# Writing out TensorE's loop over pairs of experts while the other engines keep theirs

## The chip, the cores and the metric

The kernel runs on one core of a Trainium2 chip. Five engines work side by side, each with its own list of instructions: TensorE (PE) multiplies, the vector engine (DVE), the scalar engine (ACT) and GpSimd (POOL) do elementwise work, and SyncE (SP) issues the DMA transfers. They wait for each other by semaphores. The metric is the device time of one execution in microseconds (us), as the median of several runs.

## The reference: what is computed

One inference step of a decoder with two layers, on 256 prompt tokens and 8 sample tokens (264 columns). Layer 0 is a state-space mixer and a dense SwiGLU; layer 1 is windowed attention and a mixture of experts. The change lies in the mixture alone, which takes most of the time:

```python
def moe_swiglu(h, w_router, w_gu, w_down):
    logits = jnp.einsum('btd,de->bte', h, w_router, preferred_element_type=jnp.float32)
    top_v, top_i = lax.top_k(logits, TOP_K)            # 2 of 8
    gates = jax.nn.softmax(top_v, axis=-1)
    comb = ...                                          # gates spread over the 8 experts
    for e in range(N_EXPERTS):
        out = out + comb[..., e:e + 1] * swiglu(h, w_gu[e], w_down[e])
```

The model width is 1024, an expert's hidden width 3584, everything is in 32-bit floats.

## The kernel before, in words

Each float of a weight is split into a high part (ACT's cast, line 662) and a low part (DVE's subtraction, line 1204), and TensorE makes three passes (lines 1715 to 1717) in place of one. Weights come in tiles of 128 x 2048 floats (1 MB): 51 for everything before the experts (the dense stage), then 42 for each of 8 experts, 28 for gate and up and 14 for down. SP loads a tile into one of six raw buffers once the tile six before it has been split (line 336, the function `load`). ACT casts it once TensorE has used the tile three before it (semaphore `used`), DVE subtracts after each half of the cast (`hi_made`), and TensorE multiplies after each half of the subtraction (`tiles_split`).

An expert works on at most 128 tokens. The tokens of two experts are gathered together (`gather`, line 1944, by matrices that DVE makes), which is why experts go in pairs. Then come seven blocks j of 4 tiles each for gate and up; after the second tile of block j TensorE transposes the activations of block j-1 (`turn`, line 1957). Then come 14 tiles of the down product. The result is added to the residual by `scatter` (line 1970), eight matmuls after the second and eight after the fourth tile of the next expert's block 0.

`expert_rest(r, half, more, next_pair)` is one expert from its block 1 on, and ends with block 0 of expert r+1 with the scatter of r in it. So the first block of expert 0 stands ahead of everything, and a pass of the pair loop begins at block 1 of an even expert. Its end, the border spoken of below, lies between the last scatter matmul of block 0 and the first product of block 1. The stage is three passes of that loop (experts 0 to 5), and the last pair written out after it. TensorE (line 2030), ACT (line 908) and DVE (line 1499) each have this loop for themselves; SP has one over single experts (line 349). The engines are tied by semaphores only, nothing makes them meet at a loop's end. A semaphore's target in the stage is worked out in a register from the expert's number r, by `snap`. If an expert has over 128 tokens, a further loop behind the stage takes the rest (line 2037); it is jumped over here.

In the dense stage TensorE has a smaller loop (line 1751), three passes of six tiles with 48 matmuls each.

Of the kernel before, what the change touches and what calls it, by code (L numbers as in the profile page):

```python
# [52 lines left out]
E, DFE = 8, 3584  # L53
# [26 lines left out]
def build(nc, xT, xu, gu, vecs, wd, we, wr, a_re, a_im, log_dt, bq, bx, cq, cx, h0q, h0x,  # L80
          kcT, vc, sinks, relb, onehot,
          yT, hp_out, hs_out, kp_out, vp_out, ks_out, vs_out):
    with ExitStack() as ctx:
# [7 lines left out]
        def sem(name):  # L91
            if name not in sems:
                sems[name] = ctx.enter_context(nc.semaphore(name))
            return sems[name]
# [176 lines left out]
        def expert_tile(r, m):  # L271
            return (r, NE, NDENSE + m)
# [1253 lines left out]
        def _(pe):  # L1526
# [293 lines left out]
            def turn(u):  # L1820
                pe.wait_ge(sem("p_ready"), u + 1)
                pe.wait_ge(sem("p2_ready"), heads_upto(u))
                if u >= 2:
                    pe.wait_ge(sem("pt_ready"), u - 1)
                for i in range(3 if UNITS[u] < NH else 1):
                    mm = t_.transpose(ps[:, 2 + u % 2, i * P:(i + 1) * P], SC[:, u % 3, i * P:(i + 1) * P], ident[:, :])
                mm.then_inc(sem("p_turned"), 1)
# [109 lines left out]
            def gather(r, i, experts):  # L1937

                if i == 0:
                    pe.wait_ge(sem("dispatched"), pe.snap(r * 3 + 3 * experts))  # L1940
                for c in range(2):
                    for t in range(3):
                        for part in (HTH, HTL):
                            mm = t_.matmul(ps[:, i, c * 2 * P:(c + 1) * 2 * P],  # L1944
                                           part[:, t, (2 * i + c) * P:(2 * i + c + 1) * P], DSP[:, t, :],
                                           start=(t == 0 and part is HTH), stop=(t == 2 and part is HTL))
                mm.then_inc(sem("gathered"), experts)
# [13 lines left out]
            def scatter(r, i):  # L1961

                if i == 0:
                    pe.wait_ge(sem("ye_split"), pe.snap(r + 1))
                    pe.wait_ge(sem("gs_made"), pe.snap(r + 1))
                else:
                    pe.wait_ge(sem("x_added"), pe.snap(r * 2 + 2))
                for c in range(4 * i, 4 * i + 4):
                    for y in (YEH, YEL):
                        mm = t_.matmul(ps[:, 4 + c % 4, 0:NT], y[:, c * P:(c + 1) * P], GSH[:, :],  # L1970
                                       start=(y is YEH), stop=(y is YEL))
                mm.then_inc(sem("scattered"), 1)

            def product(tile, stat, bank, first, last):

                w = WH[tile[2] % SPLIT], WL[tile[2] % SPLIT]
                for k in range(2):
                    pe.wait_ge(split, at(pe, tile, 1, 2) if k else half_of(pe, tile))
                    for i in range(2):
                        cols = slice((2 * k + i) * 512, (2 * k + i + 1) * 512)  # L1980
                        mm = passes(ps[:, bank + i, :], stat[k], [x[:, cols] for x in w],
                                    first and k == 0, last and k == 1)
                mm.then_inc(used, 1)

            def expert_gate_up(r, j, half, experts=0, prev=None):
                if j >= 2:
                    pe.wait_ge(sem("act_ready"), pe.snap(r * JE + (j - 1)))
                slots = slice(half * P, (half + 1) * P)
                for kq in range(4):
                    if experts and j == 0 and kq:  # L1990
                        pe.wait_ge(sem("xel_ready"), pe.snap(r * 4 + experts * (kq + 1)))
                    elif experts and j == 0:
                        pe.wait_ge(sem("xel_ready"), pe.snap(r * 4 + experts * 2))
                    product(expert_tile(r, 4 * j + kq), [[x[:, 2 * kq + k, slots] for x in (XEH, XEL)] for k in range(2)],
                            2 * (j % 2), kq == 0, kq == 3)
                    if kq == 1 and j:
                        turn(r, j - 1)
                    if prev is not None and kq % 2:
                        scatter(prev, kq // 2)

            def expert_rest(r, half, more, next_pair=False):
                for j in range(1, JE):
                    expert_gate_up(r, j, half)
                for d in range(NDE):
                    if d % 2 == 0:
                        pe.wait_ge(sem("af_split"), pe.snap(r * JE + (d // 2 + 1)))
                    product(expert_tile(r, NGU + d), [[x[:, 2 * d + k, :] for x in (AFH, AFL)] for k in range(2)],
                            4, d == 0, d == NDE - 1)
                    if d == 1:
                        turn(r, JE - 1)  # L2010
                    if d == 3:

                        pe.wait_ge(sem("af_split"), pe.snap(r * JE + (JE - 1)))
                        pe.wait_ge(sem("gate_spread"), pe.snap(r * 3 + 3))
                        for t in range(3):
                            mm = t_.transpose(ps[:, 7, t * P:(t + 1) * P], DG[:, t, :], ident[:, :])
                        mm.then_inc(sem("gate_turned"), 1)
                    if 5 <= d < 9 and next_pair:
                        gather(pe.snap(r + 1), d - 5, 2)
                if more:  # L2020
                    expert_gate_up(pe.snap(r + 1), 0, 1 - half, 2 if next_pair else 0, r)
                else:
                    scatter(r, 0)
                    scatter(r, 1)

            zero = pe.snap(0)
            for i in range(4):
                gather(zero, i, 2)
            expert_gate_up(zero, 0, 0, 2)
            with pe.Fori(0, E // 2 - 1) as p:  # L2030
                expert_rest(pe.snap(p * 2), 0, True)
                expert_rest(pe.snap(p * 2 + 1), 1, True, True)
            expert_rest(pe.snap(zero + (E - 2)), 0, True)
            expert_rest(pe.snap(zero + (E - 1)), 1, False)
            pe.wait_ge(sem("plan_ready"), 1)
# [90 lines left out]
```

## Time and profile before

| what | value |
|---|---|
| median of 3 runs | 1606.36 us (1605.78 to 1606.58) |
| profiled execution | 1608.89 us, span 1606.8 us |
| TensorE busy | 1506.1 us, 94% |
| TensorE weight loads busy | 1275.2 us, 79% |
| DVE busy | 1257.1 us, 78% |
| ACT busy | 999.1 us, 62% |
| data read from HBM | 415.31 MB, 263 GB/s over the span |
| mean granted TensorE clock | 0.969 |

A profile is one execution; its span runs from the first to the last instruction. PE are the matmuls and PEld the weight loads that overlap them; PEldq, DVEq and ACTq are what an engine's sequencer handles by itself, such as register operations and branches. Times in rows are us from the span's start unless marked ns. The duration of a matmul is longer than the distance to the next, since matmuls are pipelined; distances are read from starts. "[3.65 <-DVE WL L1204]" is the idle time of the engine ahead of an instruction, and what the profile takes for its end.

### The profile page before, as it was taken

How to read it: one execution, taken by the hardware profiler on the slowest of the kernel's cores; microseconds unless marked ns; L12 is line 12 of the kernel's file. 1: busy time of each engine (PE TensorE's matmuls, PEld its weight loads, DVE VectorE, ACT ScalarE, POOL GpSimd, SP SyncE). 2: the span in 40 equal slices, each digit the busy share in tenths (PEclk: the TensorE clock that was granted, in tenths of full speed). 3: DMA queues.
4: the chain of work that ended last, by engine and by line, in shares of the span. 5: the costliest groups of instructions: out<-in, count | busy, mean ns of one | idle time of the engine just before them, and what ended most of it. 6: DMA issues, size and time to landing. Idle time of an engine off the chain costs nothing.

```text
span 1606.8 us, 23615 instructions
## 1 busy us (share of the span) xinstructions
PE 1506.1 (94%) x8293; PEld 1275.2 (79%) x8294; DVE 1257.1 (78%) x1532; ACT 999.1 (62%) x1315; POOL 121.1 (8%) x143
## 2 busy tenths in 40 slices
PE   2799989999898899999999999999999999999995
PEld 1788989999777688888878888887888888888884
DVE  7964565554566489899979989988989989999983
ACT  4444444433456467777757777776777777777772
POOL 3982003000100000000000000000000000000000
PEclk9798999999899999999999999999999999999997
DMA  2005588445413259999988999988999988999980
GB/s 103 27 1 200 204 131 309 177 171 183 152 58 139 79 227 362 368 354 364 348 308 324 360 366 351 360 312 311 361 370 346 363 328 336 361 367 356 364 320 28
DMA packets 61948, 423.68 MB, mean 264 GB/s; under 512 B 8302, under 2 KB 8454, under 8 KB 11665
## 3 DMA queue, kind: packets, MB, share of 16 engines
q1 hardware_dynamic: 58784, 412.37, 67.7%
q0 software_dynamic: 3056, 9.85, 3.0%
q8 instruction: 69, 1.13, 0.3%
q14 instruction: 39, 0.32, 0.1%
HBM read 415.31 MB, written 6.88 MB: 263 GB/s over the span
## 4 chain that ended last, share of the span: by engine, by line
PE 89%; DVE 7%; ACT 2%; issue 1%; DMA 0%; SPq 0%; DVEq 0%; ACTq 0%
PE ps L1715 26%; PE ps L1717 26%; PE ps L1716 26%; PE ps L1944 2%; PE ps L1957 2%; PE ps L1532 1%; PE ps L1596 1%; PE ps L1970 1%; PE ps L1627 1%; PE ps L1628 1%; PE ps L1568 1%; DVE XN L978 0%; ACT TM L625 0%; PE ps L1576 0%; DVE AM L1081 0%
## 5 line engine op out<-in xcount | busy, mean ns | idle before, releaser
L1204 DVE TENSOR_TENSOR WL<-raw,WH 128x1024 fp32r<-128x1024 f32 x774 | 908.0, 1222 | 120.7 <-ACT WH L662 120.0
L662 ACT CAST WH<-raw 128x1024 fp32r<-128x1024 f32 x774 | 772.3, 1047 | 176.4 <-PE ps L1717 176.3
L1715 PE MATMUL ps<-WH,XEH 128*128 128x512 f32 x896 | 361.1, 403 | 7.3 <-DVE WL L1204 7.3
L1717 PE MATMUL ps<-WH,XEL 128*128 128x512 f32 x896 | 353.3, 394 | 0.0
L1716 PE MATMUL ps<-WL,XEH 128*128 128x512 f32 x896 | 352.8, 394 | 0.0
L1715 PEld LDWEIGHTS ps<-WH,XEH 128*128 128x128 f32 x896 | 168.7, 188 | 44.1 <-DVE WL L1204 7.8
L1717 PEld LDWEIGHTS ps<-WH,XEL 128*128 128x128 f32 x896 | 169.1, 189 | 42.9
L1716 PEld LDWEIGHTS ps<-WL,XEH 128*128 128x128 f32 x896 | 169.0, 189 | 36.7
L1715 PE MATMUL ps<-WH,AFH 128*128 128x512 f32 x448 | 178.8, 399 | 0.0
L1717 PE MATMUL ps<-WH,AFL 128*128 128x512 f32 x448 | 176.7, 394 | 0.0
L1716 PE MATMUL ps<-WL,AFH 128*128 128x512 f32 x448 | 176.6, 394 | 0.0
L1715 PE MATMUL ps<-XNH,WH 128*128 128x264 f32 x496 | 145.7, 294 | 9.7 <-DVE XNL L973 9.7
L1716 PE MATMUL ps<-XNL,WH 128*128 128x264 f32 x496 | 143.6, 290 | 0.0
L1717 PE MATMUL ps<-XNH,WL 128*128 128x264 f32 x496 | 143.5, 289 | 0.0
L1715 PEld LDWEIGHTS ps<-XNH,WH 128*128 128x128 f32 x496 | 96.6, 195 | 10.8 <-issue 10.5
L1717 PEld LDWEIGHTS ps<-WH,AFL 128*128 128x128 f32 x448 | 84.1, 188 | 20.8
L1716 PEld LDWEIGHTS ps<-WL,AFH 128*128 128x128 f32 x448 | 84.2, 188 | 18.9
L1715 PEld LDWEIGHTS ps<-WH,AFH 128*128 128x128 f32 x448 | 84.2, 188 | 18.9
L1716 PEld LDWEIGHTS ps<-XNL,WH 128*128 128x128 f32 x496 | 96.8, 195 | 0.2
L1717 PEld LDWEIGHTS ps<-XNH,WL 128*128 128x128 f32 x496 | 96.2, 194 | 0.0
L871 ACT CAST AFH<-ps 128x512 fp32r<-128x512 f32 x56 | 32.9, 587 | 67.7 <-PE ps L1957 67.7
L723 ACT ACTIVATE SG<-ps 128x264 f32<-128x264 f32 x30 | 11.7, 390 | 91.7 <-PE ps L1717 91.6
(368 smaller groups left out, 1772.2 us busy)
## 6 DMA issues: line engine op xcount, KB each, us to landing
raw<-in_we SPq DMA_DIRECT2D x336, 1024.0 KB, 5.3
raw<-in_wd SPq DMA_DIRECT2D x51, 1024.0 KB, 4.8
bias_rows<-SC POOLq DMA_DIRECT2D x1, 3072.0 KB, 35.7
BIAS<-bias_rows POOLq DMA_DIRECT2D x16, 128.0 KB, 9.7
U<-in_xu SPq DMA_DIRECT2D x1, 1280.0 KB, 7.8
X<-in_xT SPq DMA_DIRECT2D x1, 1056.0 KB, 10.7
out_yT<-XN SPq DMA_DIRECT2D x2, 528.0 KB, 2.7
out_ks<-KCT POOLq DMA_DIRECT2D x1, 1024.0 KB, 9.3
```

The lines of the kernel that those rows point to most:

```text
L662: a.copy(WH[tile[2] % SPLIT][:, cols], raw[slot_][:, cols]).then_inc(sem("hi_made"), 1)
L871: a.copy(AFH[:, 4 * j:4 * j + 4, :], ps[:, 6 + j % 2, :].rearrange("p (c n) -> p c n", c=4))\
L1204: v.tensor_tensor(WL[tile[2] % SPLIT][:, cols], raw[tile[2] % RING][:, cols], WH[tile[2] % SPLIT][:, cols].bitcast(F32), ALU.subtract).the ...
L1532: t_.matmul(ps[:, NORM_BANK[i], 0:NT], ones[:, :], SQ[:, c % 2, :], start=(c == 0), stop=(c == KC - 1))\
L1568: mm = t_.matmul(ps[:, 6 + b % 2, g * UC:(g + 1) * UC], AT[:, 4 * (b % 2) + g, :], U[:, hf * GH + 4 * b + g, :], start=True, stop=True)
L1596: mm = t_.matmul(ps[:, 2 + b % 2, g * P:(g + 1) * P], AM[:, hf * GH + 4 * b + g, :], CM[hf][:, 4 * b + g, :], start=True, stop=True)
L1627: t_.matmul(out, U[:, 4 * u + g, :], TM[hf][:, k, :], start=True, stop=False)
L1715: t_.matmul(out, sh, mh, start=first, stop=False)
L1716: t_.matmul(out, sh, ml, start=False, stop=False)
L1717: return t_.matmul(out, sl, mh, start=False, stop=last)
L1944: mm = t_.matmul(ps[:, i, c * 2 * P:(c + 1) * 2 * P], part[:, t, (2 * i + c) * P:(2 * i + c + 1) * P], DSP[:, t, :], start=(t == 0 and par ...
L1957: mm = t_.transpose(ps[:, 6 + j % 2, i * P:(i + 1) * P], AC[:, j % 2, i * P:(i + 1) * P], ident[:, :])
```

## The change: the loop is written out on TensorE

```diff
@@ -2027,9 +2027,9 @@
             for i in range(4):
                 gather(zero, i, 2)
             expert_gate_up(zero, 0, 0, 2)
-            with pe.Fori(0, E // 2 - 1) as p:
-                expert_rest(pe.snap(p * 2), 0, True)
-                expert_rest(pe.snap(p * 2 + 1), 1, True, True)
+            for p in range(E // 2 - 1):
+                expert_rest(pe.snap(zero + 2 * p), 0, True)
+                expert_rest(pe.snap(zero + (2 * p + 1)), 1, True, True)
             expert_rest(pe.snap(zero + (E - 2)), 0, True)
             expert_rest(pe.snap(zero + (E - 1)), 1, False)
             pe.wait_ge(sem("plan_ready"), 1)
```

`pe.Fori` is a loop that runs on the engine's sequencer, with a counter in a register and a jump back at its end. The Python loop writes its body three times into TensorE's list. `zero` is a register that holds 0. TensorE executes the same matmuls and waits in the same order; ACT, DVE and SP are as they were.

## Rows read from the trace of the kernel before

**Rows 1.** The page, part 4: the chain that ended last, by engine.

```profile
PE 89%; DVE 7%; ACT 2%; issue 1%; DMA 0%; SPq 0%; DVEq 0%; ACTq 0%
```

**Rows 2.** Waits of PE, 572 to 1590 us: total us, times, longest.

```profile
PE ps L1715 <- DVE WL L1204: 7.3, 2, 3.7
PE ps L1970 <- DVE YEL L1465: 2.5, 1, 2.5
PE ps L1970 <- DVE X L1445: 1.4, 1, 1.4
```

**Rows 3.** Timeline of PE, first pass's end: start, us, instruction, idle before.

```profile
833.98 0.28 PE L1970 MATMUL ps<-GSH,YEL 128*128 128x264 f32 x1
837.91 0.49 PE L1715 MATMUL ps<-WH,XEH 128*128 128x512 f32 x1 [3.65 <-DVE WL L1204]
...
845.14 0.60 PE L1957 MATMUL ps<-ident,AC 128*128 128x128 f32 x4
```

**Rows 4.** The same at the second pass's end.

```profile
1090.37 0.28 PE L1970 MATMUL ps<-GSH,YEL 128*128 128x264 f32 x1
1094.34 0.62 PE L1715 MATMUL ps<-WH,XEH 128*128 128x512 f32 x1 [3.69 <-DVE WL L1204]
...
1101.57 0.60 PE L1957 MATMUL ps<-ident,AC 128*128 128x128 f32 x4
```

**Rows 5.** The same at the third pass's end, and two later tiles' first matmuls.

```profile
1346.84 0.28 PE L1970 MATMUL ps<-GSH,YEL 128*128 128x264 f32 x1
1346.95 0.39 PE L1715 MATMUL ps<-WH,XEH 128*128 128x512 f32 x1
...
1352.53 0.60 PE L1957 MATMUL ps<-ident,AC 128*128 128x128 f32 x4
...
1355.76 0.39 PE L1715 MATMUL ps<-WH,XEH 128*128 128x512 f32 x1
...
1358.54 0.39 PE L1715 MATMUL ps<-WH,XEH 128*128 128x512 f32 x1
```

**Rows 6.** Line 2030, TensorE's pair loop: ns min/median/max, first and last start.

```profile
L2030 PEldq COMPARE_BRANCH  x3: 83/5919/5973, 831.8 to 1344.7; - x3
```

**Rows 7.** Busy time by stretch: us, PE, PEld, DVE, ACT, POOL, PEclk, DMA share, GB/s.

```profile
838.50:841.90 3.40, 3.40 (x10) 2.65 (x9) 0.00 (x0) 0.00 (x0) 0.00 (x0) 0.51 0.80 304
1352.50:1580.00 227.50, 226.79 (x1015) 183.42 (x1013) 202.86 (x188) 167.34 (x185) 0.00 (x0) 1.00 0.86 332
846.00:1090.00 244.00, 244.00 (x1117) 198.94 (x1117) 222.01 (x218) 182.53 (x206) 0.00 (x0) 1.00 0.92 350
```

**Rows 8.** Timeline of PE, the first pass's first transposes.

```profile
588.73 0.60 PE L1957 MATMUL ps<-ident,AC 128*128 128x128 f32 x4
```

**Rows 9.** DMA queues, 834 to 1090, then 1346 to 1580: transfers, MB, share.

```profile
q8 instruction: 12, 0.20, 0.3%
...
q8 instruction: 8, 0.13, 0.2%
```

**Rows 10.** Line 1751, TensorE's loop in the dense stage, as in rows 6.

```profile
L1751 PEldq COMPARE_BRANCH  x3: 83/220/247, 248.0 to 317.6; - x3
```

**Rows 11.** Timeline of ACT, first cast behind the first and third border.

```profile
842.55 2.00 ACT L662 CAST WH<-raw 128x1024 fp32r<-128x1024 f32 x2 [6.74 <-PE ps L1717]
...
1349.99 2.00 ACT L662 CAST WH<-raw 128x1024 fp32r<-128x1024 f32 x2 [1.32 <-PE ps L1717]
```

**Rows 12.** Line 1499, DVE's pair loop, in 836:842 and in 1092:1098.

```profile
L1499 DVEq COMPARE_BRANCH  x1: 63/63/63, 836.0 to 836.0; - x1
L1499 DVEq FUSED_REGOPS  x1: 80/80/80, 840.3 to 840.3; - x1
...
L1499 DVEq FUSED_REGOPS  x1: 74/74/74, 1096.6 to 1096.6; - x1
```

**Rows 13.** Timeline of DVE behind the third border, next three tiles (two halves each).

```profile
1351.20 2.35 DVE L1204 TENSOR_TENSOR WL<-raw,WH 128x1024 fp32r<-128x1024 f32 x2
...
1354.73 4.73 DVE L1204 TENSOR_TENSOR WL<-raw,WH 128x1024 fp32r<-128x1024 f32 x4 [0.25 <-ACT WH L662]
```

## The prediction

> **What bounds the kernel now.** I read the page's chain of waits first: 89% of the span is TensorE, 7% DVE [rows 1], so only what shortens TensorE's own line of matmuls can shorten the kernel. Then the list of waits, cut to the expert stage and to TensorE, for what interrupts that line: three entries, 11.2 us in all, of some 1,000 us [rows 2]. Two of the interruptions, 7.3 us together, stand before line 1715, at the first matmul of a tile; the other two (2.5 and 1.4 us) are the exposed last scatter of the last expert, which the change does not touch.
>
> The timeline shows where the two are. The last scatter matmul of the first pass starts at 833.98 and the next matmul at 837.91, 3.93 us later; in the second pass it is 1090.37 and 1094.34, 3.97 us [rows 3, 4]. The same place at the end of the third pass, where the loop is left by falling through, has 1346.84 and 1346.95: 0.11 us [rows 5]. The same instructions, the same queues; the loop's jump back is what two of the three have. The rows of line 2030, the loop itself, say it directly: three branches on TensorE's sequencer, of 83, 5919 and 5973 ns (minimum, median, maximum) [rows 6]. The sequencer reaches the branch ahead of the array (at 831.8 by that view), so some 2 us of the 5.9 pass under matmuls already queued and the rest is the gap. The profile's releaser, DVE's WL, is only the last semaphore that this tile waited for, given long before: in the third pass the same wait costs nothing.
>
> There is a second price. [...] So I measure an edge not by its gap but from the last scatter matmul to the first group of transposes (line 1957), two tiles later, when the clock is back: 845.14 - 833.98 = 11.16 us, 1101.57 - 1090.37 = 11.20 us, and without a jump 1352.53 - 1346.84 = 5.69 us [rows 3 to 5]. An edge costs 5.47 and 5.51 us, 10.98 us together, of which 3.82 and 3.86 are the gap and 1.65 each the slow clock.
>
> Is any of it made good later, so that it would not be a gain? From the transposes to the next pass's last scatter the kernel takes 833.98 - 588.73 = 245.25 us in the first pass (no jump ahead of it), 1090.37 - 845.14 = 245.23 in the second and 1346.84 - 1101.57 = 245.27 in the third [rows 3 to 5, 8]. Nothing is made good: the stall comes off whole.
>
> **The change, part by part.** Removed: TensorE's two taken jumps. By the above 10.98 us, all on the path. The third branch (83 ns, not taken) and the loop's counter go too; the sequencer runs ahead there (the gap is 0.11 us), so nothing.
>
> Added: the expert number as `zero + 2p` instead of `2p`. It stays a register, and every wait goes on being computed from it; the last pair has this form already and runs at TensorE's pace: its stretch from 1352.5 to 1580 has 226.79 us of 227.50 busy at clock 1.00 [rows 7]. Nothing, with no visible end on either side but the 0.7 us of that row for a whole pair.
>
> Moved: the instructions come from new code instead of from the same code again. Both are fetched anyway. The second pass of the loop has 12 transfers of the instruction queue q8, the straight last pair 8 in a stretch a little shorter (1346 to 1580 against 834 to 1090) [rows 9]. TensorE runs 288 matmuls in a pass of the dense loop (line 1751), about 1,150 in a pass of this one; only this one pays at its edge, while that loop's branches take 83 to 247 ns [rows 10]. The large loop is read anew in each pass, so writing it out adds no transfers worth a term, and straight code crosses from one transfer to the next without a gap in [rows 7]. Bounds: nothing, or for some 20 transfers in two passes up to the 0.7 us of the last pair each time, 1.4 us. I take nothing, since the passes of 245.2 us contain such transfers and agree to 0.04 us.
>
> What is late next. ACT and DVE keep their loops, and TensorE's pause covered their jumps. ACT: its first cast behind the first border starts at 842.55 after 6.74 us of idle time, put down to TensorE, which frees the buffer; in the third pass the same cast waits 1.32 us for the same [rows 11]. Hence ACT's jump costs between 0 and 6.7 us, and up to 1.3 us of it are hidden in any case; I take it as hidden, since TensorE explains the idle time by itself. DVE is the tighter one. Its branch is at 836.0 and its loop's next instruction, the counter's, at 840.3; in the second pass the counter is at 1096.6, 6.2 us behind the last scatter as against 6.3 us [rows 12, 3, 4]. So its jump costs 4.2 us, and it can start the next WL at some 840.3 + 0.1 - 833.98 = 6.4 us behind the last scatter, where in the third pass it starts at 1351.20 - 1346.84 = 4.36 us [rows 13, 5]: 2.1 us later. Its slack in the third pass: that WL's first half is there at 1351.20 + 1.2 = 1352.4 and TensorE wants it at 1355.76 (the tile's first matmul), 3.3 us; the next tile's at 1354.73 + 1.2 = 1355.9 against 1358.54, 2.6 us [rows 5, 13]. With 2.1 us gone 1.2 and 0.5 us remain, and TensorE doesn't wait. If the whole slack were gone, each us more of DVE's jump would be a us of TensorE; from below the cost is nothing. I take 0.1 us for each edge, for a fetch a little slower when TensorE's loads run on beside it.
>
> SP: with no pause its loads follow without one. A stretch of 244 us between two borders runs at a DMA share of 0.92, the last pair at 0.86 [rows 7], and TensorE, which would be the last to feel a late load, waits for nothing in them [rows 2]. Nothing; if loads did fall behind in a longer run, it would be a loss of the same kind as DVE's, below.
>
> At the end the branch of line 2037 and the final norm stand as before, behind all this.
>
> Sum against the profiled execution (1608.89 us): 10.98 - 0.2 = 10.8 us less, 1598.1 us. The median shown, 1606.36, is 2.53 us below the profiled one; on it the forecast is 1595.6 us.
>
> **The rivals.**
> DVE's loop edge takes over in part. For: DVE is busy 202.86 us of 227.5 [rows 7] and can't catch up fast; its slack is 0.5 us by my count. Against: the half us is there. Price: were its jump as long as TensorE's 5.97 us instead of 4.2, the 1.75 us more would exceed the 0.5 by 1.2 us, at two edges 2.5 us. Time 1606.36 - 10.98 + 2.5 = 1597.9 us; with TensorE's clock falling again after such a wait (1.65 each) 1601.2.
>
> The change doesn't remove what costs: the gap is the wait for WL, as the profile's releaser says, and the jump is cheap, as at the dense loop's edge (0.25 us at most [rows 10]). Then two jumps save at most 0.5 us: 1605.9 us. For it speak the releaser and those branches. Against it: the third pass, and branches of 5.9 us in [rows 6]. [...]
>
> Slower: TensorE's unbroken run grows from some 480 us (1101.6 to the end, at clock 1.00 [rows 7]) to some 1,000 us. If the granted clock fell to half somewhere in it, each us there would cost half a us; it decides from 28 us at half clock on (10.98 + 3.2, doubled). At 40 us: 1606.36 - 10.98 + 20 = 1615.4 us. Nothing in the trace hints at it: the only falls in this stage follow a standstill.
>
> **How the numbers follow.** About 0.2%, 3.2 us, is what a measurement of this kernel can tell from no change. The forecast 0.86; DVE's edge in part 0.07; the jump not the cause 0.04; slower by the clock 0.02; a mixture that loses over half the gain 0.01. The first two, and half of the last, are faster by over 0.2%: 0.94; within 0.2%: 0.04; slower: 0.02. Range: down to 1593.6 (the gain whole, and 1.8 us for another run's level; the three runs of before span 0.8 us), up to 1599.6 (beyond DVE's case, 1597.9). The other signs hold too little chance to widen it.
>
> **What the changed kernel's profile would show.** At the pair borders, near 834, 1085 and 1336 us, the next matmul 0.1 us behind the last scatter and the transposes at 5.7 us, with no clock below 1.00 there: the term of 10.98. TensorE's waits in the stage down to the two of the last expert, 3.9 us. No branch rows on its sequencer at the loop. DVE still with its jump of 4.2 us, its next WL at about 6.4 us, and TensorE's tile at 8.9 us without a wait: the term of 0.1. I am wrong if gaps of us stay at those borders (the cause was the data), if TensorE waits two or three tiles behind them (DVE's edge), if gaps appear every 20 us within a pair (fetching), or if the clock falls in mid-run.

## The result, and the profile after

The changed kernel takes 1594.35 us in the median (1593.03 to 1595.24, four runs) against 1606.47 us, 12.1 us less: a ratio of 0.9921, 95% interval 0.9908 to 0.9934, which is 10.6 to 14.8 us. (The ratio, here and below, is an estimate of its own; that of the two medians would be 0.9925.) The forecast was 1595.6 us. The profiled execution took 1593.03 us with a span of 1590.9, against 1608.89 and 1606.8 before.

The chain of waits of the page is as before. TensorE's waits between 572 and 1580 us, the columns as in [rows 2], no longer hold an entry for line 1715; the two of the last expert's scatter are left (the first line is the final norm, behind the stage).

```profile
PE ps L1532 <- ACT SQ L534: 4.6, 1, 4.6
PE ps L1970 <- DVE YEL L1465: 2.5, 1, 2.5
PE ps L1970 <- DVE X L1445: 1.3, 1, 1.3
```

TensorE's timeline at the first border answers to [rows 3], and below it the one stretch of busy time (columns as in [rows 7]) that spans the whole stage.

```profile
828.96 0.28 PE L1970 MATMUL ps<-GSH,YEL 128*128 128x264 f32 x1
829.08 0.39 PE L1715 MATMUL ps<-WH,XEH 128*128 128x512 f32 x1
...
834.65 0.60 PE L1957 MATMUL ps<-ident,AC 128*128 128x128 f32 x4
```

```profile
567.00:1563.00 996.00, 996.00 (x4538) 810.99 (x4536) 904.36 (x884) 740.18 (x828) 0.00 (x0) 1.00 0.92 346
```

The border takes 5.69 us where [rows 3] have 11.16; at the second it is 1085.57 - 1079.87 = 5.70 us. TensorE is busy for 996 of 996 us at a granted clock of 1.00. The loop's rows of line 2030 are gone with the loop, and q8, the queue of the instructions, moves 63 transfers in the whole kernel in place of 69.

DVE's side of the first border, its timeline and the rows of its loop, answers to [rows 12, 13]:

```profile
832.16 1.25 DVE L1445 TENSOR_TENSOR X<-ps,X 128x1056 f32<-128x1056 f32 x1
835.27 2.36 DVE L1204 TENSOR_TENSOR WL<-raw,WH 128x1024 fp32r<-128x1024 f32 x2 [1.85 <-issue]
```

```profile
L1499 DVEq COMPARE_BRANCH  x1: 62/62/62, 831.0 to 831.0; - x1
L1499 DVEq FUSED_REGOPS  x1: 80/80/80, 835.1 to 835.1; - x1
```

Its next WL starts 835.27 - 828.96 = 6.31 us behind the last scatter, now with its own jump ("issue") named for the idle time and no longer ACT, and TensorE does not wait for it.

A measure without the scatter of whole runs. The profiles' spans differ by 15.9 us, more than the medians. The difference lies in two parts: ahead of the expert stage, where no instruction was changed, and in it. The first and last start of TensorE's gather (line 1944) and scatter (line 1970), in ns min/median/max and us, for the kernel before and then for the changed one:

```profile
L1944 PE MATMUL ps<-DSP,HTH x96: 276/283/582, 564.0 to 1319.7; 128*128 128x256 f32 x96
L1970 PE MATMUL ps<-GSH,YEL x64: 278/284/425, 698.4 to 1586.3; 128*128 128x264 f32 x64
```

```profile
L1944 PE MATMUL ps<-DSP,HTH x96: 276/283/582, 559.1 to 1303.6; 128*128 128x256 f32 x96
L1970 PE MATMUL ps<-GSH,YEL x64: 278/283/422, 693.4 to 1570.1; 128*128 128x264 f32 x64
```

From the first gather to the last scatter, "the stage" from here on, the kernel before takes 1586.3 - 564.0 = 1022.3 us and the changed one 1570.1 - 559.1 = 1011.0: 11.3 us. Another 564.0 - 559.1 = 4.9 us stand ahead of it, where the mean granted clock of the first 558 us is 0.94 before and 0.96 after; behind the last scatter the changed kernel takes 0.3 us more.

### The profile page after: what moved, and what is told of

Same layout as the page of the kernel before. It is cut to its first block, busy times and chain, and to the rows that moved or that the text cites. A ratio compares the mean times of both kernels' runs of the same rounds, so it can differ in the third digit from the quotient of the medians.

```text
span 1590.9 us, 23128 instructions
## 1 busy us (share of the span) xinstructions
PE 1496.5 (94%) x8293; PEld 1267.1 (80%) x8294; DVE 1256.6 (79%) x1532; ACT 999.5 (63%) x1315; POOL 121.5 (8%) x143
## 4 chain that ended last, share of the span: by engine, by line
PE 89%; DVE 7%; ACT 3%; issue 1%; DMA 0%; SPq 0%; DVEq 0%; ACTq 0%
PE ps L1715 26%; PE ps L1717 26%; PE ps L1716 26%; PE ps L1944 2%; PE ps L1957 2%; PE ps L1532 1%; PE ps L1970 1%; PE ps L1596 1%; PE ps L1627 1%; PE ps L1628 1%; PE ps L1568 1%; DVE XN L978 0%; ACT TM L625 0%; DVE SV L1113 0%; PE ps L1576 0%
## 5 line engine op out<-in xcount | busy, mean ns | idle before, releaser
L662 ACT CAST WH<-raw 128x1024 fp32r<-128x1024 f32 x774 | 772.3, 1047 | 165.2 <-PE ps L1717 165.1
L1715 PEld LDWEIGHTS ps<-XNH,WH 128*128 128x128 f32 x496 | 95.6, 193 | 11.3 <-issue 10.5
```

Of the source, the lines that this page charges most:

```text
L662: a.copy(WH[tile[2] % SPLIT][:, cols], raw[slot_][:, cols]).then_inc(sem("hi_made"), 1)
L1715: t_.matmul(out, sh, mh, start=first, stop=False)
```

## The experiments

The stage's length is given for each from the same two rows of its own profile, beside the timed median. All ratios are to the kernel before, timed anew beside each group of experiments: 1606.81 us for the first four, 1607.07 us for the four with a hint, with far jumps or with a placed head, 1606.41 us for the other four.

**The changed kernel once more.** No edit.

> The changed kernel once more, beside the others on the same chip. The forecast was 10.8 us less than before, the first measurement 12.1 us (ratio 0.9908 to 0.9934, 10.6 to 14.8 us). Theory A (the two jumps of TensorE cost 5.5 us each and nothing else changed; the rest of the first profile's 15.9 us is scatter of the granted clock ahead of the expert stage): 1595.5 us, a saving of 10.5 to 12 us, and a profile whose time between the first gather and the last scatter is 11 us shorter than before's, wherever the stage starts. Rival B (something ahead of the expert stage got faster too, through the new layout of TensorE's code): a saving of 13 us or more, and the stage starting at 567 us again in the profile, not at 572.

Measured: 1595.42 us (1592.16 to 1595.54), ratio 0.9922, interval 0.9910 to 0.9935: a saving of 11.4 us between the medians, 12.5 us by the ratio. The stage takes 1569.4 - 558.5 = 1010.9 us. It starts at 558.5 here, and at 563.9 in the kernel below that has all loops written out and the same code ahead of the stage: the start wanders by 5.4 us among kernels whose code there is the same. The first profiles' difference of 4.9 us is of that size. Theory A holds by the stage; rival B falls, since a start at 564 us occurs with the new layout too.

**One pass written out.**

```diff
-            with pe.Fori(0, E // 2 - 1) as p:
+            expert_rest(pe.snap(zero), 0, True)
+            expert_rest(pe.snap(zero + 1), 1, True, True)
+            with pe.Fori(1, E // 2 - 1) as p:
```

> Only the first of TensorE's three passes is written out, the other two stay a loop, so one jump back is left. Theory A: a saving of 5.5 us (1601 us), the first border with a gap of 0.1 us, the second with 3.8 us and the granted clock at half for some 3.4 us behind it. Rival (the loop form or the register for the expert number costs something in each pass, not the jump): a saving of a third of the whole, 3.7 to 4 us, or of two thirds. Rival (DVE's late start at the border costs TensorE something that was hidden so far): under 5 us.

Measured: 1603.57 us (eleven runs, 1600.03 to 1608.48), ratio 0.9983, interval 0.9972 to 0.9993: 3.2 us saved between the medians where 5.5 were expected. The stage takes 1578.5 - 558.7 = 1019.8 us, 2.5 less than before. The written-out border is clean, as expected; the one that is left costs more than it did. TensorE's timeline there, and the granted clock behind it:

```profile
1079.49 0.28 PE L1970 MATMUL ps<-GSH,YEL 128*128 128x264 f32 x1
1083.63 0.79 PE L1715 MATMUL ps<-WH,XEH 128*128 128x512 f32 x1 [3.86 <-DVE WL L1204]
1088.56 0.80 PE L1717 MATMUL ps<-WH,XEL 128*128 128x512 f32 x1 [1.16 <-issue]
1094.14 0.60 PE L1957 MATMUL ps<-ident,AC 128*128 128x128 f32 x4
```

```profile
1082.30:1092.50 10.20, 7.71 (x17) 5.63 (x18) 2.39 (x3) 1.82 (x2) 0.00 (x0) 0.50 0.46 169
```

The border takes 14.65 us, 8.96 more than without a jump. There is a second stop, in the middle of a tile, that waits for nothing but "issue", and the clock is at half for 10.2 us in place of 3.4; it fell 1.3 us before TensorE resumed. My theory gave the right sign and the wrong size: an edge has no fixed price. A share of the whole in proportion to the passes (the rival, 3.7 to 4 us) would not be far from 3.2 us either, but the timeline shows the cost at the one border and none at the other, so it is not that.

**The other engines' loops written out, TensorE's kept.** The edit of the change, made on ACT (line 908) and DVE (line 1499) in place of TensorE.

> ACT's and DVE's loops are written out, TensorE keeps its own: the change the other way about. Theory A: TensorE's jumps of 5.9 us stay on the path, so no change within 0.1% (1606 us), both gaps of 3.8 us stay, while DVE's idle time at the border is put down to ACT alone. Rival (the gap was the wait for the split weights, as the profile's releaser says, because DVE's own jump made it late): the gaps at the borders shrink and most of the 11 us are saved here too, 1596 us.

Measured: 1606.38 us, ratio 0.9997, interval 0.9989 to 1.0006; the stage 1583.1 - 560.7 = 1022.4 us. TensorE's rows at the loop and at the first border:

```profile
L2030 PEldq COMPARE_BRANCH  x3: 76/5810/6067, 828.5 to 1341.3; - x3
```

```profile
830.63 0.28 PE L1970 MATMUL ps<-GSH,YEL 128*128 128x264 f32 x1
834.71 0.49 PE L1715 MATMUL ps<-WH,XEH 128*128 128x512 f32 x1 [3.80 <-DVE WL L1204]
```

The gap is there with DVE's jump gone, and the profile goes on naming DVE for it. The releaser was never the cause; the rival falls.

**All three loops written out.**

> All three loops over pairs are written out. Theory A: the same as the changed kernel within 0.1% (1594 to 1596 us), because DVE's start, 2.1 us late behind its jump, stays within its slack; in the profile DVE's next WL starts 4.4 us behind the last scatter at all three borders instead of 6.3. Rival (DVE's jump takes part of the gain): faster than the changed kernel by up to 2 us, 1593 us.

Measured: 1595.16 us (1593.11 to 1597.53), ratio 0.9924, interval 0.9911 to 0.9936; the stage 1575.0 - 563.9 = 1011.1 us, as against 1011.0 and 1010.9. DVE's next WL starts 838.25 - 833.88 = 4.37 us behind the last scatter, as expected, and not 6.31, and TensorE gains nothing by it. DVE's own jump costs nothing here, where its 2 us stay within its slack: the rival of the prediction, tried from its other side, is worth 0.0 us.

**The loop kept, its branch hinted.** One instruction more in each pass, at its head; the trace calls it BRANCH_PREFETCH_HINT (36 to 55 ns).

```diff
-            with pe.Fori(0, E // 2 - 1) as p:
+            with nc.Fori(0, E // 2 - 1, engines=[mybir.EngineType.PE], hint_back_edge=True) as p:
```

> [...] 
```profile
L2030 PEldq BRANCH_PREFETCH_HINT  x3: 36/36/55, 577.4 to 1080.1; - x3
L2030 PEldq COMPARE_BRANCH  x3: 87/354/382, 828.8 to 1330.6; - x3
```

The same taken jumps now cost 0.38 and 0.35 us, where they cost 5.92 and 5.97. This is the decisive run: the loop, its counter, its registers and its jumps are all there, and all of the gain is there as well. What cost was waiting for the jump's target to be fetched, and not the number of fetches: q8 moves 68 transfers here, one less than before. Read from the DMA view in steps of 0.1 us, one starts at 820.5 and the next at 832.9, and the branch between them, at 828.8, is over in 0.38 us; in the kernel before, the branch starts at 831.8, a transfer at 835.3, and TensorE's next matmul at 837.91. The same view bears on what the hint does. In the 8 us from the first taken branch on, q8 starts two transfers in the kernel before (835.3 and 838.5) and one here (832.9), and from the second on two and one again; from the third branch on, which is not taken, it starts none in the kernel before and one here, at 1334.3. That fits a target fetched ahead of the branch (820.5 is 8.3 us ahead) in place of the code that follows in line. The view does not say which code a transfer holds.

**Jumps put into the written-out kernel,** over never executed matmuls, in front of the second and third pass.

```diff
+            pe.wait_ge(sem("plan_ready"), 1)
+            spare = pe.value_load(plan[0:1, 4 * E:4 * E + 1], min_val=E, max_val=E + 4)
...
+                if p < 2:
+                    with pe.If(spare > E):
+                        for _ in range((300, 1200)[p]):
+                            t_.matmul(ps[:, 7, 0:P], ident[:, :], ident[:, :], start=True, stop=True)
```

> The written-out loop, with a jump forward in front of the second and of the third pass, over 300 and over 1200 matmuls that are never executed (each with its weight load; the condition is read once from the plan). Theory A: the jump over 1200 lands in code that is not there and costs a gap of 2 to 4 us and, if the clock falls, 5.5 us; the one over 300 costs as much if what is fetched ahead reaches less far than 600 instructions. Stage some 5.5 or 11 us longer than 1010.9. Rival (only jumps back, with the loop's counter, stall): no gap at either.

> As the kernel with far jumps, but the never executed matmuls at the two borders are 8 (16 instructions with their weight loads) and 100 (200 instructions). The jump over 300 matmuls cost as much as the loop's jump back, a branch of 6.07 us. Theory A: the jump over 16 instructions lands in the block that is running and costs nothing, the one over 200 lands in that block or the next, which is there; both branches 0.1 to 0.4 us, no gap, first gather to last scatter 1011 us, 1595.5 us. If only the running block were there, the second would cost its 4 to 6 us. Rival (each taken jump drains the queue): gaps at both, 1022 us and 1606 us.

Measured, 300 and 1200 matmuls: 1607.39 us, ratio 1.0000 (0.9991 to 1.0010), the stage 1585.4 - 563.8 = 1021.6 us. With 8 and 100: 1595.98 us, ratio 0.9927 (0.9911 to 0.9943), the stage 1573.2 - 562.1 = 1011.1 us. The branches of the two kernels, far ones first:

```profile
L2036 PEldq COMPARE_BRANCH  x2: 5883/5978/6072, 831.4 to 1087.7; - x2
```

```profile
L2036 PEldq COMPARE_BRANCH  x2: 329/341/353, 829.8 to 1080.7; - x2
```

A jump forward is as dear as the loop's jump back (5.92 and 5.97 us) if it goes over 600 instructions (6.07 us), and costs 0.33 us over 200. Between 300 and 1200 matmuls (5.88 us) it does not get dearer. The rivals (only a loop stalls; every taken jump stalls) fall, one by each kernel.

**Where the loop's head lies.** After the surprise of the second stop, theory C: the code comes in blocks of 256 instructions. [rows 9] bear it out roughly, by an estimate: 8 transfers for the straight pair's 1,047 matmuls and as many weight loads are about 260 instructions each.
```diff
+            with nc.Fori(1, E // 2 - 1, engines=[mybir.EngineType.PE], head_slot={mybir.EngineType.PE: 0}) as p:
...
+            with nc.Fori(0, E // 2 - 1, engines=[mybir.EngineType.PE], head_slot={mybir.EngineType.PE: 232}) as p:
```

> The kernel with one pass written out, whose one jump cost 8.8 us in place of 5.5: TensorE stood a second time, 1.79 us, 3.15 us after it had resumed, and the clock stayed at half for 10.2 us. New theory C (the code is fetched in blocks of 256 instructions; its loop's head lay near a block's end, so that the next block was needed before it had come): with the head placed on the first slot of a block, the second gap goes, the edge costs 5.5 us again, and first gather to last scatter takes 1016.4 us in place of 1019.8. Rival (the longer half clock was chance, or DVE's late start caused the second gap): second gap and 1019 to 1020 us again.

> The kernel before, its loop's head moved to slot 232 of a block of 256. Theory C: both edges get the second gap of 1 to 2 us, some 10 to 12 matmuls behind the first, and cost 7 to 9 us each in place of 5.5: first gather to last scatter 1025 to 1030 us in place of 1022.3, some 1609 to 1613 us. Rival (the place of the head does not matter): 1022.3 us and 1606.5 us as before.

Measured, head at 0: 1600.40 us, ratio 0.9961 (0.9947 to 0.9975); the stage 1577.0 - 559.5 = 1017.5 us. The second stop is gone; the border takes 1092.52 - 1080.38 = 12.14 us, 6.45 more than without a jump, where 5.5 were expected. The stop is no longer than before (3.52 us idle); what is longer is the spell at half clock, 6.7 us in place of 3.4:

```profile
1083.30:1090.00 6.70, 5.83 (x14) 4.58 (x15) 1.53 (x2) 0.31 (x1) 0.00 (x0) 0.50 0.67 264
```

Head at 232: 1606.86 us, ratio 1.0002 (0.9992 to 1.0012), the stage 1584.2 - 560.5 = 1023.7 us where 1025 to 1030 were expected. Its two borders:

```profile
830.38 0.28 PE L1970 MATMUL ps<-GSH,YEL 128*128 128x264 f32 x1
834.90 0.79 PE L1715 MATMUL ps<-WH,XEH 128*128 128x512 f32 x1 [4.23 <-issue]
...
840.55 0.50 PE L1717 MATMUL ps<-WH,XEL 128*128 128x512 f32 x1 [1.29 <-issue]
843.68 0.60 PE L1957 MATMUL ps<-ident,AC 128*128 128x128 f32 x4
...
1088.93 0.28 PE L1970 MATMUL ps<-GSH,YEL 128*128 128x264 f32 x1
1092.69 0.49 PE L1715 MATMUL ps<-WH,XEH 128*128 128x512 f32 x1 [3.48 <-DVE WL L1204]
...
1095.69 0.50 PE L1717 MATMUL ps<-WH,XEL 128*128 128x512 f32 x1 [0.19 <-issue]
1098.83 0.60 PE L1957 MATMUL ps<-ident,AC 128*128 128x128 f32 x4
```

Both have the second stop, 11 matmuls behind the border, which with their weight loads are 22 instructions, about the 24 slots that are left in the block. At the first border it is 1.29 us long, and the border takes 13.30 us, 7.61 more than without a jump. At the second it is 0.19 us, and the clock does not fall: 9.90 us in all, 4.21 more. So in these profiles theory C holds for where the second stop comes and for whether it comes, and not for its length. The transfers of q8 fit it. The next block's starts at 838.1 us at the first of these borders, at 1093.4 at the second, and at 1086.1 in the kernel with one pass written out, 5.8, 3.4 and 5.1 us behind the one for the jump's target; TensorE goes on 2.3 to 2.5 us later. With the head at slot 0 that transfer starts at 1084.9, and nothing in it is needed so soon. Why it starts late at one border and not at the other stays open.

**The border moved between two tiles.** The loop stays. Its body begins one block of gate and up later, and that block is issued ahead of the loop for expert 0 and at the end of `expert_rest` for the next.

```diff
-                for j in range(1, JE):
+                for j in range(2, JE):
...
                     expert_gate_up(pe.snap(r + 1), 0, 1 - half, 2 if next_pair else 0, r)
+                    expert_gate_up(pe.snap(r + 1), 1, 1 - half)
...
+            expert_gate_up(zero, 1, 0)
```

> The loop stays, but its border is moved by one block of gate and up, from behind the eight short scatter matmuls (0.12 us each) to between two full products (0.23 us each). The sequencer was some 13 matmuls ahead of the array at its branch, 2.2 us of work. Theory A (a fixed fetch of 5.9 us, of which only what is queued is hidden): with 13 matmuls of 0.23 us queued 3.0 us are hidden, the gap falls from 3.8 to 3.0 us, an edge from 5.5 to 4.7 us, first gather to last scatter 1020.7 us. Rival (the array stops for a fixed time at a jump): 3.8 us and 1022.3 us again. The transposes of the block may come right behind the border or not; DVE's loop keeps its border, so its late start now falls elsewhere.

Measured: 1597.24 us, ratio 0.9940 (0.9925 to 0.9955), the stage 1574.8 - 561.1 = 1013.7 us: 8.6 us less with both jumps in place, where I expected 1.6. The gap did fall, but the branch fell too, and that was no part of my theory. The branch rows, the tile behind the first border, and the DMA of the time from that branch on (columns as in [rows 7]):

```profile
L2032 PEldq COMPARE_BRANCH  x3: 76/3335/3788, 839.9 to 1343.1; - x3
```

```profile
843.55 0.50 PE L1715 MATMUL ps<-WH,XEH 128*128 128x512 f32 x1 [0.61 <-issue]
```

```profile
839.90:840.90 1.00, 1.00 (x6) 0.80 (x5) 1.00 (x2) 0.71 (x1) 0.00 (x0) 1.00 0.00 0
```

The same for the kernel before, from its first branch at 831.8 on:

```profile
831.80:835.30 3.50, 2.46 (x15) 1.98 (x13) 3.26 (x4) 2.71 (x4) 0.00 (x0) 1.00 0.98 405
```

At the moved border the DMA engines are idle when the branch is reached (share 0.00), and q8's transfer starts at 840.9, 1.0 us behind the branch. At the old border they are busy with weights (share 0.98, 405 GB/s), and it starts at 835.3, 3.5 us behind the branch. From there to the first product it is 2.6 us in both (843.55 and 837.91), so the difference lies in when the transfer starts. The second borders agree: the transfer starts 1.0 us behind the branch at 1092.1 (share 0.00 until 1093.0), and 3.5 behind the one at 1088.2 (share 1.02). Branches of 3.3 to 3.8 us with no load ahead, and of 5.8 to 6.4 with loads under way, are what all far jumps of TensorE in these runs have: ten at the old border with 5.8 to 6.4, two here with 3.3 and 3.8, and those at line 2037 (2039 to 2044 in kernels with more lines) with 3.3 to 3.9, where no load is under way (share 0.02 to 0.03). I did not move the loads alone, so that the loads are the cause is a reading that fits, not one shown by itself.

**The other far jump taken off the path.** DVE and TensorE get the common case first, with the final norm in it; the jump over the rare case comes behind. Then the same with the hinted loop.

```diff
+            with dve.If(any_more < E + 1):
+                dve.drain()
+                v.memset(cnt[:, 0:1], 0.0).then_inc(sem("moe_done"), 1)
+                norm(4, G_FIN, sem("xn_ready"))
             with dve.If(any_more > E):
...
```

The old drain, memset and norm move into the rare case's `If`, and TensorE's `norm(4)` is split in the same way.

> The changed kernel, and the other far jump that stands on the path taken off it: at the end of the stage DVE jumps over the code for experts with more than 128 tokens, and 2.87 us pass between its branch and its next instruction, for which ACT's and TensorE's final norm wait. Here the common case is written first, with the final norm in it, on DVE and TensorE, and the jump over the rare case comes behind it. Theory A: last scatter to last matmul falls from 11.7 to some 8.9 us, and the kernel from 1595.4 to 1592.6 us. Rival (ACT's start of the norm or the store at the end takes its place, or the jump behind the norm makes the end late): under 1 us.

> The same end, with TensorE's loop kept and its branch hinted in place of the loop written out. The hinted loop took 1011.08 us from first gather to last scatter against 1010.92 written out. Theory A: the same as the previous kernel within 0.1%, 1592.7 us. Rival (one hint is lost, or the hinted loop's two branches of 0.37 us count): 0.7 us more, or 5.5 us more if one edge stalls.

Measured, written out: 1593.38 us (1591.72 to 1593.59), ratio 0.9912 (0.9899 to 0.9926); the stage 1572.0 - 560.9 = 1011.1 us. Hinted: 1595.79 us, ratio 0.9929 (0.9915 to 0.9942). The end of DVE and TensorE in the changed kernel, and in the first of these:

```profile
1568.35 0.59 PE L1970 MATMUL ps<-GSH,YEH 128*128 128x264 f32 x1 [1.35 <-DVE X L1445]
...
1574.53 0.06 DVE L1521 MEMSET cnt<- 1x1 f32 x1 [2.76 <-issue]
...
1575.10 7.05 PE L1532 MATMUL ps<-SQ,ones 128*128 128x264 f32 x16 [4.62 <-ACT SQ L534]
```

```profile
1570.29 0.59 PE L1974 MATMUL ps<-GSH,YEH 128*128 128x264 f32 x1 [1.35 <-DVE X L1445]
...
1573.83 0.06 DVE L1507 MEMSET cnt<- 1x1 f32 x1
...
1574.40 6.86 PE L1536 MATMUL ps<-SQ,ones 128*128 128x264 f32 x16 [1.98 <-ACT SQ L534]
```

The norm starts 4.11 us behind the last scatter's start in place of 6.75: the 2.6 us of the jump are gone. Part is given back at the very end. The store of the output lands in 2.6 us in the changed kernel, in 4.2 and 3.8 us in these two. The jumps over the rare case now fall close to that store; that they slow it is not shown. The medians are 1.0 us below the changed kernel's first measurement (2.0 below its second) and, for the hinted one, none, with intervals that overlap: a gain over the changed kernel is not settled. The written-out one beats the kernel before by 13.0 us, the lowest median of all.

## Why the prediction was right

What bounds the kernel, and the two gaps. Right. The rival that took the releaser at its word is out by two kernels: the gap stays with DVE's jump gone, and goes with TensorE's branch hinted.

The term of 10.98 us. Right in sum: the stage lost 11.3 us. The borders lost 5.47 and 5.50, and tenths elsewhere in the stage make up the rest. It was right because it was read off this kernel's own two borders against its third. What I had not seen is that the 5.5 us are no property of a jump. Four quantities make them, each with a size of its own: the branch (0.33 to 0.38 us with the target at hand, 3.3 to 3.8 without it, 5.8 to 6.4 without it at a place where loads are under way), what is queued on TensorE and hides part of it (2.2 us before the change, from 831.8 to 833.98), the spell of half clock behind it (none to 10.2 us), and, where the head lies near the end of a block, a second stop at the next block (0.19 and 1.29 us idle with the head at 232). The 1.65 us that the sum gives to the slow clock at each border fit what the trace shows behind both: 3.4 us at a granted clock of 0.51 [rows 7] and, from 1094.5 to 1097.8, 0.51 again. With the head at slot 232 two borders of one kernel differ by 3.4 us. The forecast did not need them to be alike, since it took away the very two that it had measured. Three of my later expectations took the 5.5 us, or its branch of 5.9, for a constant and missed: 8.96 and 6.45 us for the single border left, and 8.6 us saved by moving the border where 1.6 were expected. The fourth, for the head at 232, gave every second stop 1 to 2 us and missed too.

"Nothing is made good", "the expert number costs nothing", "straight code runs without a gap". Right: 996.00 us busy of 996.00, and the hinted loop, with the old registers, has a stage within 0.2 us of the written-out one. The rival of a cheap jump had a chance of 0.04. In these runs a loop's branch takes 76 to 87 ns when it is not taken, 0.22 to 0.38 us when it is taken to code at hand, and 3.3 us and more when the target is far. That the time goes into fetching the target is what the hinted loop (0.35 and 0.38 us) and the far and near jumps (5.88 and 6.07 us against 0.33 and 0.35) bear out.

DVE's edge. Right: its WL at 6.31 us (forecast 6.4), TensorE without a wait, and 0.0 us in place of the 0.1 that I took for each edge, a term that no row had given.

The slower rival. 996 us at a granted clock of 1.00: nothing of it.

The last step, from the profiled execution to the median: the forecast takes the profiled execution to be 2.53 us above the median before and after alike. After, it was 1.3 us below; the stage's lengths are free of that. The saving in the median, 12.1 us, is 0.8 above the stage's 11.3, well within an interval of 4 us.

## What to carry to other kernels

Read a loop's edge in the rows of the sequencer, not in the releaser: here the branches of 3.3 to 6.4 us, in place of 0.1 to 0.4, were those that waited for a fetch, and the profile mostly put the gap down to the semaphore of the first instruction behind it (DVE's WL, 3.65 us in [rows 3], 3.80 us with DVE's loop written out). A hint at the loop's head gave the same as writing the loop out (a stage of 1011.1 us against 1011.0), with the body in the code once and not three times; a border where the DMA engines are idle gave 8.6 of the 11.3 us. Price such an edge from the kernel's own rows and not from another edge: moved by one block the same jump went from 5.5 to about 1.3 us, half of the 2.7 by which that stage is longer than the changed kernel's.

## What the runs showed that I had not expected

The half clock behind a stop is no fixed toll. Behind stops of 3.4 to 4.2 us it lasted 3.4 us [rows 7], 6.7 us (one pass out, head at 0), 10.2 us (one pass out), or did not come: at the second border with the head at 232 the 4.21 us in all are the stop of 3.65 and, with the second stop, tenths behind it. Behind the 0.61 and 1.40 us of the moved border it did not come either. What decides it stays open.

How far the code at hand reaches was shown in part. The dense loop's pass of 288 matmuls with their loads jumps back in 0.25 us at most [rows 10], and q8 moves nothing from 252 to 317 us while that loop runs: its code stays. The pair loop's pass, four times as long, does not: 12 transfers in its second pass [rows 9], and branches of 5.9 us. Ahead, the code behind 100 matmuls with their loads is at hand (0.33 us) and that behind 300 is not (6.07 us); where between them the limit lies, and whether it is another than the one backwards, no run here shows.
